# The gates' steps move from a stage of their own into the projection

## The reference, cut to what matters

```python
h = rmsnorm(x, norm_w)
z, xbc, dt_raw, qkv, a_raw, b_raw, gate, mg_ssm, mg_gdn = split_cols(h @ w_in, IN_SIZES)
xbc = silu(causal_dwconv(xbc) + ssm_conv_b); qkv = silu(causal_dwconv(qkv))
dt = softplus(dt_raw + ssm_dt_bias)
g = -exp(gdn_a_log) * softplus(a_raw + gdn_dt_bias)
beta = sigmoid(b_raw)
acum = cumsum(dt * A) within a chunk;  gcum = cumsum(g) within a chunk
```

## Time and profile before

| | |
|---|---|
| median of three runs | 3165.31 us |
| the profiled execution / its span | 3172.0 us / 3170.2 us |
| TensorE busy (matmuls) | 2926.8 us, 92% of the span |
| VectorE / ScalarE / GpSimd busy | 1518.6 / 1035.3 / 395.3 us |
| end of the norm's mask casts | 50.44 us |
| first matmul of the projection | 102.85 us |

### The profile page before, as it was taken

How to read it: one execution, slowest core, us unless ns; L and a number is a source line. 1 busy time by engine, 2 the same in 40 slices (tenths; PEclk the granted TensorE clock), 3 DMA queues, 4 the chain that set the end, 5 groups by cost and what they waited for, 6 DMA issues and landing times. The chain is left out here.

```text
span 3170.2 us, 50932 instructions
## 1 busy us (share of the span) xinstructions
PE 2926.8 (92%) x18908; PEld 2782.8 (88%) x18908; DVE 1518.6 (48%) x2298; ACT 1035.3 (33%) x2145; POOL 395.3 (12%) x542
## 2 busy tenths in 40 slices
PE   3799999999999989999999777999879999998998
PEld 1799999999999978878878537999879999998998
DVE  5355555531110148888888554554453233233453
ACT  3233222321121135545645243333331121123332
POOL 2000000000000022333333210000110000000100
PEclk7899999999999989999999777999989999999999
DMA  2222222222224222442443447644421212215543
GB/s 80 73 95 95 88 88 95 95 95 95 95 88 137 95 79 66 99 99 66 99 99 45 156 164 265 219 156 156 162 83 61 81 60 91 76 60 194 179 154 109
DMA packets 239560, 348.05 MB, mean 110 GB/s; under 512 B 154664, under 2 KB 174440, under 8 KB 239184
## 3 DMA queue, kind: packets, MB, share of 16 engines
q1 hardware_dynamic: 234448, 326.71, 32.6%
q0 software_dynamic: 4992, 19.78, 1.7%
HBM read 253.24 MB, written 93.22 MB: 109 GB/s over the span
## 5 line engine op out<-in xcount | busy, mean ns | idle before, releaser
L534 PE MATMUL pps<-h_hi,pwh 128*128 128x352 f32 (+1 forms) x2112 | 689.2, 326 | 15.8 <-DVE pwl L599 15.8
L534 PE MATMUL pps<-h_hi,pwl 128*128 128x352 f32 (+1 forms) x2112 | 686.3, 325 | 0.0
L534 PE MATMUL pps<-h_lo,pwh 128*128 128x352 f32 (+1 forms) x2112 | 684.5, 324 | 0.0
L534 PEld LDWEIGHTS pps<-h_hi,pwh 128*128 128x128 f32 x2112 | 397.1, 188 | 16.1 <-issue 16.1
L534 PEld LDWEIGHTS pps<-h_lo,pwh 128*128 128x128 f32 x2112 | 397.8, 188 | 0.0
L534 PEld LDWEIGHTS pps<-h_hi,pwl 128*128 128x128 f32 x2112 | 397.5, 188 | 0.0
L2355 PE MATMUL u_ps<-f_hi,up_wh 128*128 128x352 f32 (+1 forms) x1056 | 344.6, 326 | 11.0 <-DVE up_wl L2347 11.0
L599 DVE TENSOR_TENSOR pwl<-pw,pwh 128x1024 fp32r<-128x1024 f32 x88 | 107.8, 1226 | 505.0 <-ACT pwh L547 498.3
L2355 PE MATMUL u_ps<-f_hi,up_wl 128*128 128x352 f32 (+1 forms) x1056 | 344.5, 326 | 0.0
L2355 PE MATMUL u_ps<-f_lo,up_wh 128*128 128x352 f32 (+1 forms) x1056 | 343.9, 326 | 0.0
L2355 PE MATMUL merge_ps<-merge_yh,merge_wh 128*128 128x352 f32 (+1 forms) x576 | 191.5, 332 | 22.5 <-DVE merge_wl L2347 21.0
(11 more groups left out here) (453 smaller groups left out, 5158.9 us busy)
## 6 DMA issues: line engine op xcount, KB each, us to landing
projected<-pO SPq DMA_DIRECT2D x88, 536.0 KB, 3.0
pw<-in_w_in SPq DMA_DIRECT2D x88, 512.0 KB, 4.0
merge_w<-in_w_out SPq DMA_DIRECT2D x72, 512.0 KB, 3.3
down_w<-in_w_down SPq DMA_DIRECT2D x48, 704.0 KB, 4.1
up_w<-in_w_up SPq DMA_DIRECT2D x44, 512.0 KB, 4.3
scan_chunk<-projected SPq DMA_DIRECT2D x5, 2496.0 KB, 11.5
wo_w<-in_w_o SPq DMA_DIRECT2D x24, 512.0 KB, 3.3
ffn<-uf SPq DMA_DIRECT2D x22, 536.0 KB, 2.9
```

The source lines that it names most:

```text
L534: ins = pe.matmul(ps[:, 3 * u + n, 0:cn], l[u][:, k, :], r[:, k, c0:c0 + cn], start=(k == 0 and a == 0), stop=(k == KD - 1 and a == 2))
```

## The change

`gates_phase` is gone. Its steps are called `gates(engine, step)`, one set for each of TensorE, ScalarE and VectorE, and `stages` calls them ahead of every fourth silu tile: the silu tiles, one loop of 12 passes before, are six loops of two. Step 0 does the product for two column blocks, step 1 for the third, step 2 the transposes, softplus, `adt` and `beta`, step 3 the sums over the chunk and what follows from them, step 4 the sums of the running sequences and the first four turned chunks, step 5 the other seven. The gates' buffers lie in `merge_raw`, which is free until `load_first`; their products go to two PSUM banks of their own. In steps 2, 3 and 4 ScalarE loads the table of exp and ln first, and the silu table again behind.

The norm loads the projection's first two weight tiles and splits the first (ScalarE between its second exponential and second `hi`, VectorE at its end). Masks that are float32 are loaded into place, the bf16 ones are cast by ScalarE ahead of the first logarithm. In the projection SP loads the gates' weights and two rows behind the constants; VectorE raises 22 semaphores and then releases tile 0 by hand (`sem_inc(lo_done[0])`). SP writes `decay_sums` in `load_first`, and waits for it there, and for five tables.

```diff
+            cast = [(name, n, at) for name, n, dt, at in placed_masks() if dt == BF16]
+            kept = [(name, n, at) for name, n, dt, at in placed_masks() if dt == F32]
+            masks_raw = sb("c_raw", [P, sum(n for _, n, _ in cast)])
...
-                sp.dma_start(masks_raw[:, :], masks).then_inc(masks_in.sems[0], 16)
+                sp.dma_start(masks_raw[:, :], masks[:, cast[0][2]:cast[-1][2] + cast[-1][1]]).then_inc(masks_in.sems[0], 16)
+                for u in range(2):
+                    sp.dma_start(w_parts[0][:, u, :, :], w_first[u]).then_inc(first_w_in.sems[0], 16)
+                for name, n, at in kept:
+                    sp.dma_start(con[name][:, :], masks[:, at:at + n]).then_inc(kept_in.sems[0], 16)
+                sp.wait_ge(kept_in.sems[0], kept_in.at(0))
...
+                if con is not None and n == 0:
+                    act.wait_ge(masks_in.sems[0], masks_in.at(0))
+                    at = 0
+                    for name, m, _ in cast:
+                        act.activation(con[name][:, :], masks_raw[:, at:at + m], ACT.Copy)
+                        at += m
...
+                if con is not None and n == 1:
+                    act.wait_ge(first_w_in.sems[0], first_w_in.at(0))
+                    act.activation(w_parts[1][:, :, :], w_parts[0][:, 0, :, :], ACT.Copy).then_inc(first_hi.sem, 1)
...
-                dve.wait_ge(masks_in.sems[0], masks_in.at(0))
-                at = 0
-                for name, n, _ in MASKS:
-                    dve.tensor_copy(con[name][:, :], masks_raw[:, at:at + n])
-                    at += n
+                dve.wait_ge(first_hi.sem, first_hi.at(0))
+                dve.tensor_tensor(w_parts[2][:, :, :], w_parts[0][:, 0, :, :], w_parts[1][:, :, :].bitcast(F32), ALU.subtract)
...
+        def stages(eng, body, start=lambda kind: None, gates=lambda eng, step: None):
+
+            for kind, first, end in (("conv", 0, CT), *(("silu", CT + 4 * n, CT + 4 * n + 4) for n in range(6)),
+                                     ("sigmoid", NSCAN, NTILE - 2)):
+                if kind == "silu":
+                    gates(eng, (first - CT) // 4)
...
-                sp.dma_start(w[:, u, :, :], d["w_in"][u]).then_inc(w_in.sems[u], 16)
+                sp.sem_inc(w_in.sems[u], 16)
...
             sp.dma_start(old[:, :, :], d["conv_old"]).then_inc(consts_in.sems[0], 16)
+            sp.dma_start(gw, d["w_small"]).then_inc(gw_in.sems[0], 16)
+            sp.dma_start(bias, d["gate_bias"].to_broadcast([P, 48])).then_inc(rows_in.sems[0], 16)
+            sp.dma_start(alog, d["a_log"].to_broadcast([P, H])).then_inc(rows_in.sems[0], 16)
...
             def load_first(kind):
                 if kind == "sigmoid":
+                    sp.wait_ge(ev["acct_done"].sem, ev["acct_done"].at(0, 3))
+                    sp.dma_start(sums, accT[0:3 * H, :]).then_inc(sums_out.sems[0], 16)
                     for u in range(2):
                         sp.wait_ge(stored.sems[u], stored.at(NSCAN // 2 - 1))
+                    sp.wait_ge(sums_out.sems[0], sums_out.at(0))
+                    for name, k in (("weights_done", 1), ("be_done", 1), ("beta_done", 1), ("dt_done", 1), ("seq_done", 1)):
+                        sp.wait_ge(ev[name].sem, ev[name].at(0, k))
...
+            def gates(pe, step):
+                if step == 0:
+                    pe.wait_ge(ev["w_lo"].sem, ev["w_lo"].at(0, 1))
+                    gate_product(0, 0)
+                    gate_product(1, 1)
+                if step == 1:
+                    pe.wait_ge(ev["gathered"].sem, ev["gathered"].at(0, 2))
+                    gate_product(2, 0)
+                if step == 2:
+                    pe.wait_ge(ev["gathered"].sem, ev["gathered"].at(0, 3))
+                    for t in range(NCH):
+                        n = C if t < NC else TS
+                        ins = pe.transpose(gps[0:n, t // 6, (t % 6) * 48:(t % 6) * 48 + 48], by_channel[0:48, t * C:t * C + n],
...
+                    ins.then_inc(ev["raw_mm"].sem, 1)
+                if step == 3:
+                    pe.wait_ge(ev["adt_done"].sem, ev["adt_done"].at(0, 1))
+                    pe.matmul(gps[0:C, 0, 0:NC * H], con["tri"][0:C, 0:C],
+                              adt[0:C, 0:NC, :].rearrange("p t h -> p (t h)"), start=True, stop=True)
+                    pe.matmul(gps[0:TS, 0, NC * H:NCH * H], con["tri_s"][0:TS, :], adt[0:TS, NC, :], start=True, stop=True)
+                    pe.matmul(gps[0:TS, 0, NCH * H:NCH * H + H], con["same"][0:TS, :], adt[0:TS, NC, :], start=True, stop=True)
+                    pe.matmul(gps[:, 1, 0:NC * H], con["ones"][0:C, :],
...
+                if step == 4:
+                    pe.wait_ge(ev["parts_done"].sem, ev["parts_done"].at(0, 3))
+                    pe.wait_ge(ev["diff_done"].sem, ev["diff_done"].at(0, 1))
+                    for b in range(NB):
+                        ins = pe.matmul(gps[:, 1, b * H:(b + 1) * H], con["seq_wide"][0:TS, b * P:(b + 1) * P], adt[0:TS, NC, :],
+                                        start=True, stop=True)
+                    ins.then_inc(ev["seq_mm"].sem, 1)
+                    turn_sums(range(0, 4), 0)
+                if step == 5:
+                    pe.wait_ge(ev["acct_done"].sem, ev["acct_done"].at(0, 1))
+                    pe.wait_ge(ev["seq_done"].sem, ev["seq_done"].at(0, 1))
+                    turn_sums(range(4, 8), 0)
+                    turn_sums(range(8, NCH), 1)
...
+            def gates(act, step):
+                if step in (2, 3, 4):
+                    act.preload_act_table_set("natural_log_exp_and_others")
...
+                if step == 3:
+                    act.wait_ge(ev["acc_done"].sem, ev["acc_done"].at(0, 2))
+                    act.activation(tab["E"][0:C, :, :], acc[0:C, :, :], ACT.Exp).then_inc(ev["decays_done"].sem, 1)
+                    act.activation(tab["EL"][:, 0:NC, :].rearrange("p t h -> p (t h)"), gps[:, 1, 0:NC * H],
+                                   ACT.Exp).then_inc(ev["decays2_done"].sem, 1)
+                    act.wait_ge(ev["diff_done"].sem, ev["diff_done"].at(0, 1))
+                    act.wait_ge(ev["last_done"].sem, ev["last_done"].at(0, 1))
+                    act.activation(tab["W"][0:C, :, :], diff[0:C, :, :], ACT.Exp).then_inc(ev["weights_done"].sem, 1)
+                if step == 4:
+                    act.wait_ge(ev["seq_mm"].sem, ev["seq_mm"].at(0, 1))
+                    act.activation(tab["EL"][:, NC:, :].rearrange("p t h -> p (t h)"), gps[:, 1, 0:NB * H], ACT.Exp).then_inc(
+                        ev["seq_done"].sem, 1)
+                    act.wait_ge(ev["ones_set"].sem, ev["ones_set"].at(0, 1))
+                    negated(0, 0, 4 * C, 1)
...
+            act.sem_inc(hi_done[0].sem, 1)
...
+            dve.sem_inc(lo_done[0].sem, 1)
...
+            def gates(dve, step):
+                if step == 0:
...
+                    dve.memset(raw, 0.0).then_inc(ev["zeroed"].sem, 1)
+                    gathered(0, 0)
+                    gathered(1, 1)
+                if step == 1:
+                    gathered(2, 0)
...
+                if step == 3:
+                    dve.wait_ge(ev["sums_mm"].sem, ev["sums_mm"].at(0, 1))
+                    dve.tensor_copy(acc[0:C, 0:NC, :].rearrange("p t h -> p (t h)"), gps[0:C, 0, 0:NC * H]).then_inc(ev["acc_done"].sem, 1)
+                    dve.tensor_copy(acc[0:TS, NC, :], gps[0:TS, 0, NC * H:NCH * H]).then_inc(ev["acc_done"].sem, 1)
...
+                    dve.wait_ge(ev["decays2_done"].sem, ev["decays2_done"].at(0, 1))
+                    dve.tensor_tensor(diff[0:C, 0:NC, :].rearrange("p t h -> p (t h)"), gps[0:C, 1, 0:NC * H],
+                                      acc[0:C, 0:NC, :].rearrange("p t h -> p (t h)"), ALU.subtract).then_inc(ev["diff_done"].sem, 1)
...
+                if step == 4:
+                    turned(0, 0, 4 * C, 1)
...
+            dve.wait_ge(ev["w_hi"].sem, ev["w_hi"].at(0, 1))
+            dve.tensor_tensor(gwl[:, :, :], gw, gwh[:, :, :].bitcast(F32), ALU.subtract).then_inc(ev["w_lo"].sem, 1)
+            stages(dve, body, gates=gates)
...
-                with ExitStack() as to_gates:
...
-                    gates_phase(nc, d, hi, lo, tab, sums=sums, con=dict(con, seq_wide=con["seq_wide"][:, :].rearrange(
-                        "p (b q) -> p b q", b=NB)))
+                con.update({n: sb(f"c_{n}", [P, c], dt) for n, c, dt in MASKS if n in GATES_ONLY})
+                w, whi0, wlo0 = sb("pw", [P, 2, KD, P]), sb("pwh0", [P, KD, P], F32R), sb("pwl0", [P, KD, P], F32R)
+                with ExitStack() as for_norm:
+                    x = allocator(for_norm, nc)("x_T", [P, KD, T])
+                    norm_phase(nc, "mixnorm", x, d["norm_mix"], con["ones"], hi, lo, x_in=d["x"],
+                               con=con, masks=d["masks"], w_first=d["w_in"], w_parts=(w, whi0, wlo0))
...
+                project_phase(nc, d, hi, lo, scratch, sums, chunk0, con["selT"], tab, con, w, whi0, wlo0)
```

(38 more changed lines are left out.)

274 lines of the change are left out of this document (105 added, 169 removed).

## The result

The changed kernel took 3139.8 us (median of 4 runs, 3136.7 to 3142.7), the kernel before 3164.7 (median of 4): a ratio of 0.9929 with a 95% interval of 0.9916 to 0.9942, so 18 to 27 us less. Forecast were 3133 us and 32.4 us less; the time lies inside the wide range of 3126 to 3147, 6.8 us above the forecast and 0.8 above the forecast's own 3127 to 3139.

A forecast was written before the change was run, and what follows sets the result against it. TensorE was taken as the bound inside the projection, so time before its first matmul counts fully. Sum: -50.4 + 17.0 + 0.7 + 0.3 = -32.4 us, from 3165.3 to 3133 us; own range 3127 to 3139, wide range 3126 to 3147.

The forecast's parts named there:

- First product at 52.4: Start of the projection: TensorE's first matmul comes at 52.4 us, against 102.85 before; gain 50.4 us.
- The norm's pass, +0.3: Norm: ScalarE's mask casts make the first logarithm late by 0 to 1.6 us, taken as 0.3.
- Tile 0 as before, tile 1 in time: Projection's start: tile 0 takes 14.2 us as before; tile 1's weights are ready at 63.9, before tile 0 ends at 66.6.
- The gates' work, 17.0: Between silu tiles: the gates' products, transposes and sums cost TensorE their whole length at full clock, 17.0 us.
- The chain behind a step costs nothing: Silu tiles: ScalarE's and VectorE's step arithmetic before the next weight split stays hidden behind TensorE, with 1.2 us to spare.
- SP at the sigmoid tiles, 0.7: Start of the sigmoid tiles: SP's wait for the written decay sums lengthens TensorE's stall of 1.44 us by 0.7.
- Late weights: Rival, steps 2 to 4: a longer chain makes TensorE wait 2.8 us three times, 3141 us; chance 0.12.
- a late tile 1: Rival, projection's start: constants and gate weights land late, tile 1 is 4.0 us late, 3137 us; chance 0.08.
- The clock: Rival, silu tiles: each of six steps brings TensorE to 1.2 GHz, next tile 2.7 us longer, 3149 us; chance 0.06.
- New loops: Rival, silu tiles: TensorE waits for code at five additional loop entries, 10.8 us each, 3187 us; chance 0.03.

The follow-up runs named there:

- the loops alone: The kernel before with its loop over the 24 silu tiles cut in six loops of two passes, and nothing else: 3164.3 us (one run).

## Why the prediction was right, and where it was off

The mechanism came as forecast: the start gave 50.45 us, the gates' work on TensorE took 17.4 back, and nothing waited behind a step. That the time lies in the wide range is in part luck, though: it is above the forecast's own 3127 to 3139, and the room above that was meant for rivals that didn't occur. Term by term:

- *First product at 52.4*: 52.40 was measured. The gap with the six further increments grew by 3.45 - 2.66 = 0.79 us, forecast 0.7.
- *The norm's pass, +0.3*: nothing. The first logarithm still begins at 21.91.
- *Tile 0 as before, tile 1 in time*: tile 1 yes, by 9 us. Tile 0 took 14.9 us, 0.7 more, in its slow-clock stretch; in the other profiles with the early weights it took 13.9 to 14.9, and 14.2 to 14.8 in the three with the old start, so this isn't the change's own.
- *The gates' work, 17.0*: 17.4. Steps 0 and 1 hold the 72 products: 7.84 + 3.82 = 11.66, forecast 11.7.
- *The chain behind a step costs nothing*: right; TensorE waits behind none. ScalarE's load there again takes no drain. Timeline of the changed kernel, fifth step:

```profile
821.94 1.19 ACT L542 ACTIVATE pO<-pps 128x368 f32<-128x368 f32 x3 [9.62 <-PE pps L467]
823.14 1.28 ACT L486 ACT_TABLE_LOAD   x1
824.44 0.44 ACT L507 ACTIVATE t_EL<-gps 128x320 f32<-128x320 f32 x1
```

  The load begins as the evacuation ends, and the next instruction 1.30 us after the load's start. So the drain that the Trainium skill ("ScalarE: Activation LUTs", section What ACT_TABLE_LOAD costs) adds is not seen here either, and leaving it out was right.
- *SP at the sigmoid tiles, 0.7*: mis-sized; it was 3.3. The mechanism held, and the sums did land a little behind the store, 0.8 us; on the queue that made 1.2 us. I took this as the whole price. Some 0.6 of the rest are the weights' slower landing, not shown to be the change's own, and some 1.5 the clock behind the longer wait, which the term left out.
- *Not in the sum at all*: 5.7 us for the place of the weights. I listed what instructions the change adds and moves, and not what its allocations push. The masks' new lifetime stood in the diff.
- *Rivals.* Late weights and a late tile 1 didn't occur. The clock fell behind no step in the changed kernel, though in two experiments behind one, for 1.6 us and not 2.7. New loops: no stall, in the changed kernel or alone. The stall that the Trainium skill ("Runtime: NRT & Kernel Launch", section Instruction fetch mechanics) tells of is not seen at these entries: with the loops alone, the tiles there take 11.68 to 11.69 us like the others. My row for it was one tile off: the conv loop's last tile is evacuated at 666.15, and the entry lies there. No two products near 666 are over 0.19 us apart, so the reading stands, on another row than the one I named.

In the forecast's own terms, at the projection's end: 0.7 + 5.7 + 0.4 + 2.6 - 0.3 = 9.1 us too much gain, and 32.4 - 23.3 = 9.1. By the medians the gain was 24.9, and the error 7.5.

## What to carry to other kernels

When a change makes a buffer live longer, work out where the buffers behind it come to lie, and keep what TensorE reads at the offset it had; in this kernel 352 unused bytes were worth 6 us. When something is put ahead of a large transfer on a queue, price the wait at the end of that queue, with the clock behind it, and try another queue. A stage of short dependent operations ahead of a long run of products can be spread through that run: of the 46 us that it and the mask casts held, TensorE's own work came back, 17 us.

## What the runs showed of the hardware

- Products whose split weights begin 32 bytes beyond a multiple of 128 were 0.6% slower, 11.753 against 11.687 us for 72 of them, in six profiles each. At a multiple of 64 only, 11.73 to 11.76, differing from loop to loop of one kernel; why is open.
- At the sigmoid tiles, waits of 3.30 to 3.54 us in six profiles were each followed by some ten products at the lower clock (some 1.5 us more; granted 0.58 in the changed kernel's window), though not always from the first product on. Waits of 0.92, 1.38, 1.44 and 2.24 us were followed by none.
- Behind the same short products, with no wait before or after them, the granted clock stayed at 1.00 in nine profiles and was 0.57 and 0.61 over 4 us in two.
